# A transformer block in fp32 on one core: the first 352 columns of the input projection taken token tile by token tile

## The chip, the core and the metric

One NeuronCore of a Trainium2 chip runs the kernel. The metric is device time in microseconds (us), the median of the runs shown. Engines: TensorE (PE; its weight loads are PEld), VectorE (DVE), ScalarE (ACT), GpSimd (POOL) and SyncE (SP), each with a queue of its own; DMAs are issued from the queues of SP and ACT.

## What is computed

One hybrid encoder block on x of 1024 tokens by 1024 features, all in fp32. The part that matters here is its beginning:

```python
h = rms_norm(x, norm_mix_pre[l])          # per token: x * rsqrt(mean(x^2) + eps) * gain
z = h @ w_in[l]                           # 1024 x 1024 by 1024 x 2816
# columns of z: attention q (512), k (128), v (128); retention q, k, v, gate (512 each)
a = window_attention(rope(aq), rope(ak), av, attn_sink[l])
r = retention(rq, rk, rv, rg, ...)
x = x + rms_norm(concatenate([a, r]) @ w_out[l], norm_mix_post[l])
```

Behind it come cross-attention into 256 memory tokens and a SwiGLU feed-forward layer, which the change leaves alone.

## The kernel before

Tokens lie in 8 tiles of 128 (`NT`), features in 8 tiles of 128 (`NK`). A product in fp32 accuracy is made of three matmuls in the reduced fp32r format (`three`, lines 495 to 497): both operands are split into a high part (rounded) and a low part (the rest), and hi by hi, hi by lo and lo by hi are added up in PSUM. PSUM has 8 banks of 128x512.

The normalized x must be transposed before it can be the stationary operand. For a token tile t: ScalarE sums the squares (line 833) and takes the root (835), VectorE inverts it (1145) and scales the tile (1165), TensorE transposes eight 128x128 blocks into two PSUM banks (`turn_rows`, 491), ScalarE copies them out as `t_hi` (`hi_parts`, 843), VectorE subtracts for `t_lo` (`lo_parts`, 1152). x lies in the first 1024 columns of `z`, which the projection later overwrites.

The projection's 2816 columns are done in 8 pieces (`ZP`) of 352 columns (`ZW`). Per piece the 8 weight tiles (128x352) pass through a ring of four slots (`RING`): SP loads `raw` (341), GpSimd makes `w_hi` (398) and `w_lo` (402), TensorE multiplies. `product` goes weight tile by weight tile (k outside) and within it over the 8 token tiles, each with a bank of its own; so a piece can start only when all 8 token tiles are transposed and split, and it holds all 8 banks. ScalarE evicts the banks at the piece's end (876). The order is hand-written: each engine runs its own list, and semaphores tie them (`w_loaded` per slot, `w_rounded`, `w_split`, `w_used`, `tile_done`, `turned`, `act_ev`, `dve_ev`, `scaled`).

SP's queue begins with x tile 0, four weight tiles, x tiles 1 to 7. ScalarE issues the nine loads of constants (862 to 872) behind the last high part of x.

## Time and profile before

| | us |
|---|---|
| median of 3 runs | 1686.9 |
| the runs | 1686.15, 1686.9, 1692.22 |
| span of the profiled execution | 1681.7 |

The profiled execution's span runs from its first to its last instruction; what lies around it is in the runs' times and not in the span. Its mean granted TensorE clock was 0.968 of full. The page gives the busy time of each engine over the span, and the same in 40 slices. The timeline gives instructions in order of time, with the idle time before one and what ended it in brackets. Matmul ends are modelled and overlap, so the spacing of the starts is what counts, not the durations. The windows view gives busy time and granted clock of a stretch. The chain view follows back what ended last.

### The profile page before, as it was taken

To read this page: it belongs to the slowest core of one execution; us is meant where nothing else is said; L and a number is where in the kernel's file an instruction comes from. 1 tells how busy PE (TensorE), PEld (TensorE's weight loads), DVE (VectorE), ACT (ScalarE), POOL (GpSimd) and SP (SyncE) were. 2 spreads that over 40 slices of the span, in tenths; PEclk is the share of its full clock that TensorE was granted. 3 is DMA by queue.
4 is the path that set the end of the run, shared out by engine and by line. 5 is a ranking of instruction groups with operands and counts; after the bars stand their busy time and mean duration, and the time that the engine had idled before them with its cause. 6 is when DMAs were issued, how large, how long until landed. Compare 5 with 4: busy or idle time off the path is not lost.

```text
span 1681.7 us, 20944 instructions
## 1 busy us (share of the span) xinstructions
PE 1597.8 (95%) x7656; PEld 1329.0 (79%) x7656; DVE 584.5 (35%) x1022; ACT 373.2 (22%) x814; POOL 690.4 (41%) x580
## 2 busy tenths in 40 slices
PE   5999999899979999998998999999999999999995
PEld 4999999678968777875686788888888888888884
DVE  5061075455850820024138103214124042141237
ACT  5001014445432651133045100101101001011013
POOL 2444452200646575420356444434343434343435
PEclk7999999699979999999998999999999999999998
DMA  5111111000041042100011111111111111111112
GB/s 195 50 45 50 47 44 39 1 1 1 13 174 65 26 150 101 44 32 1 29 48 38 44 44 50 45 50 44 50 44 50 44 50 44 50 44 47 46 31 100
DMA packets 57236, 86.96 MB, mean 52 GB/s; under 512 B 5600, under 2 KB 36576, under 8 KB 57184
## 3 DMA queue, kind: packets, MB, share of 16 engines
q1 hardware_dynamic: 53312, 75.52, 14.6%
q10 hardware_dynamic: 3872, 10.76, 1.8%
q8 instruction: 31, 0.51, 0.1%
q14 instruction: 21, 0.17, 0.0%
HBM read 82.06 MB, written 4.19 MB: 51 GB/s over the span
## 4 chain that ended last, share of the span: by engine, by line
PE 91%; DVE 3%; ACT 3%; issue 1%; POOL 1%; DMA 0%; POOLq 0%; DVEq 0%; ACTq 0%
PE ps L495 26%; PE ps L496 26%; PE ps L497 25%; PE ps L491 4%; PE ps L614 3%; PE ps L588 3%; PE ps L760 2%; PE ps L671 1%; PE ps L649 1%; ACT px L1078 1%; DVE t_lo L1152 1%; DVE px L1400 1%; DVE wmx L1390 0%; PE ps L738 0%; DVE z L1165 0%
## 5 line engine op out<-in xcount | busy, mean ns | idle before, releaser
L398 POOL TENSOR_TENSOR w_hi<-raw,zero 128x512 fp32r<-128x512 f32 (+1 forms) x244 | 242.0, 992 | 719.9 <-PE ps L497 713.3
L495 PE MATMUL ps<-t_hi,w_hi 128*128 128x512 f32 x832 | 330.1, 397 | 4.2 <-DVE t_lo L1152 1.6
L496 PE MATMUL ps<-t_lo,w_hi 128*128 128x512 f32 x832 | 329.8, 396 | 0.0
L497 PE MATMUL ps<-t_hi,w_lo 128*128 128x512 f32 x832 | 329.8, 396 | 0.0
L402 POOL TENSOR_TENSOR w_lo<-raw,w_hi 128x512 fp32r<-128x512 f32 (+1 forms) x244 | 304.5, 1248 | 19.1
L495 PE MATMUL ps<-w_hi,t_hi 128*128 128x352 f32 (+1 forms) x768 | 268.1, 349 | 4.6 <-DVE t_lo L1152 3.1
L496 PE MATMUL ps<-w_lo,t_hi 128*128 128x352 f32 (+1 forms) x768 | 268.2, 349 | 0.0
L497 PE MATMUL ps<-w_hi,t_lo 128*128 128x352 f32 (+1 forms) x768 | 267.6, 348 | 0.0
L495 PEld LDWEIGHTS ps<-t_hi,w_hi 128*128 128x128 f32 x832 | 156.7, 188 | 43.2 <-DVE t_lo L1152 1.8
L1437 DVE TENSOR_TENSOR gs<-gs,ps 128x512 f32<-128x512 f32 x44 | 30.3, 688 | 451.4 <-ACT gs L1116 407.6
L497 PEld LDWEIGHTS ps<-t_hi,w_lo 128*128 128x128 f32 x832 | 156.7, 188 | 38.2
L496 PEld LDWEIGHTS ps<-t_lo,w_hi 128*128 128x128 f32 x832 | 156.7, 188 | 38.0
L1116 ACT ACTIVATE gs<-ps 128x512 f32<-128x512 f32 x44 | 26.3, 599 | 645.0 <-PE ps L497 645.0
L495 PEld LDWEIGHTS ps<-w_hi,t_hi 128*128 128x128 f32 x768 | 145.7, 190 | 18.0 <-DVE t_lo L1422 2.2
L497 PEld LDWEIGHTS ps<-w_hi,t_lo 128*128 128x128 f32 x768 | 145.5, 189 | 11.5
L496 PEld LDWEIGHTS ps<-w_lo,t_hi 128*128 128x128 f32 x768 | 145.5, 189 | 11.5
L1464 DVE TENSOR_TENSOR y<-ps,y 128x512 f32<-128x512 f32 x160 | 109.7, 691 | 87.9 <-PE ps L497 86.8
L496 PE MATMUL ps<-w_lo,f_hi 128*128 128x512 f32 x352 | 139.9, 397 | 0.0
L495 PE MATMUL ps<-w_hi,f_hi 128*128 128x512 f32 x352 | 138.9, 395 | 0.5 <-POOL w_lo L402 0.5
L497 PE MATMUL ps<-w_hi,f_lo 128*128 128x512 f32 x352 | 138.5, 394 | 0.0
L450 POOL TENSOR_TENSOR x<-x,y 128x1024 f32<-128x1024 f32 x24 | 57.3, 2386 | 73.1 <-DVE y L1356 73.1
L495 PEld LDWEIGHTS ps<-w_hi,f_hi 128*128 128x128 f32 x352 | 66.1, 188 | 17.6 <-POOL w_lo L402 0.9
(154 smaller groups left out, 1743.7 us busy)
## 6 DMA issues: line engine op xcount, KB each, us to landing
raw<-in_ffn_w_gu_dram SPq DMA_DIRECT2D x88, 256.0 KB, 3.1
raw<-in_w_in_dram SPq DMA_DIRECT2D x64, 176.0 KB, 2.3
raw<-in_ffn_w_down_dram SPq DMA_DIRECT2D x44, 256.0 KB, 2.6
raw<-in_xa_wkv_dram SPq DMA_DIRECT2D x32, 256.0 KB, 3.2
z<-in_x_dram SPq DMA_DIRECT2D x8, 512.0 KB, 8.1
raw<-in_w_out_dram SPq DMA_DIRECT2D x16, 256.0 KB, 2.6
x<-in_x_dram ACTq DMA_DIRECT2D x8, 512.0 KB, 8.0
raw<-in_xa_wq_dram SPq DMA_DIRECT2D x16, 256.0 KB, 2.7
```

The lines of the kernel that those rows point to most:

```text
L398: nc.gpsimd.tensor_tensor(hi[:, s, 0:width], raw[:, s, 0:width], zero[:, 0:1].broadcast_to([P, width]), ALU.add).then_inc(w_rounded, 1)
L402: nc.gpsimd.tensor_tensor(lo[:, s, 0:width], raw[:, s, 0:width], hi[:, s, 0:width].bitcast(F32), ALU.subtract).then_inc(w_split, 1)
L450: nc.gpsimd.tensor_tensor(x1[:, t, :], x1[:, t, :], y[:, t, :], ALU.add).then_inc(added, 1)
L491: return nc.tensor.transpose(ps[:, b, col:col + P], src, ident[:, :])
L495: nc.tensor.matmul(out, a_hi, b_hi, start=start, stop=False)
L496: nc.tensor.matmul(out, a_hi, b_lo, start=False, stop=False)
L497: return nc.tensor.matmul(out, a_lo, b_hi, start=False, stop=stop)
L588: nc.tensor.matmul(ps[:, j, 0:(k1 - k0) * P], qT[g * AD:(g + 1) * AD, j, n * P:(n + 1) * P], kT[g * AD:(g + 1) * AD, k0 * P:k1 * P], start ...
L614: last = nc.tensor.matmul(ps[:, 7, h * AD:(h + 1) * AD], pTw[:, j, kb * P:(kb + 1) * P], z[:, k0 + kb, C_V + g * AD:C_V + (g + 1) * AD], s ...
L760: last = nc.tensor.matmul(ps[:, 6 + d % 2, :], vM[:, mm, d * P:(d + 1) * P], pTx[:, mm, d // 2, :], start=mm == 0, stop=mm == NM - 1)
L1437: nc.vector.tensor_tensor(gs[:, p, :], gs[:, p, :], bank(2 * p + 1), ALU.mult).then_inc(dve_ev, 1)
L1464: nc.vector.tensor_tensor(v, bank(t), v, ALU.add).then_inc(dve_ev, 1)
```

## The change

The first piece (columns 0 to 351) is taken out of the loop and goes token tile by token tile. It needs all 8 weight tiles on chip at once: weight tiles 0 to 3 are split into a second ring, `w_hi3`/`w_lo3`, laid over room that is free at that time, and tiles 4 to 7 into the usual ring. Their raw data: tiles 0 to 3 in `raw`, tiles 4 to 7 in unused columns of `z`. SP loads all 8 weight tiles ahead of x tiles 1 to 7. ScalarE rounds them (it was GpSimd), GpSimd only subtracts. x is transposed through banks 4 to 7, and the first piece's tiles take banks 0 to 3 in turn, evicted by ScalarE as they are done (`first_out`, counted by `z0_out`). ScalarE starts with a Sqrt of a constant. The second piece is written out ahead of the loop, which now runs from 2. VectorE subtracts tile 0's low parts at once and those of the others one tile late, as before. The loads of constants on ScalarE's queue stay behind its x work, which now holds the evictions of the first piece too.

```diff
@@ -62,7 +62,7 @@
 TURNED = dict(x=0, qk=16, c=42, mem=58, h2=62, k=78, h3=82)
-ACT_EV = dict(x=0, z=16, qk=80, c=93, o=109, mem=125, h2=129, kv=145, k=153, q=157, xo=173, h3=189, end=205)
+ACT_EV = dict(x=0, z=8, qk=72, c=85, o=101, mem=117, h2=121, kv=137, k=145, q=149, xo=165, h3=181, end=197)
 DVE_EV = dict(x=0, qk=16, c=29, mem=45, h2=49, h3=65, end=81)
 TILES = dict(z=0, o=56, kv=70, q=74, xo=88, f=102)
@@ -77,6 +77,8 @@
 def turn_bank(n):
+    if n < TURNED["qk"]:
+        return 4 + n % 4
     if n < TURNED["mem"]:
         return (n - (TURNED["c"] if n >= TURNED["c"] else 0)) % 8
     return 4 + (n - (TURNED["h3"] if n >= TURNED["h3"] else TURNED["h2"] if n >= TURNED["h2"] else TURNED["mem"])) % 4
@@ -199,6 +201,7 @@
         Z = overlay(
             [("z", [P, NT, IN_COLS], F32), ("ropet", [P, 2 * NT * (AD // 2 + RD // 2)], F32),
              ("rope_a", [P, D], F32), ("rope_b", [P, D], F32)],
+            [("z_3", [P, NT, IN_COLS], F32), ("w_hi3", [P, RING, 512], F32R), ("w_lo3", [P, RING, 512], F32R)],
             [("z_1", [P, NT, IN_COLS], F32), ("junk_c", [P, 1536], F32), ("qtab", [P, RH, 2, P], F32),
              ("pTw", [P, G, 3 * P], F32)],
             [("z_2", [P, NT, IN_COLS], F32), ("junk_d", [P, 1536], F32), ("qtab_1", [P, RH, 2, P], F32),
@@ -233,10 +237,12 @@
         w_loaded = [sem(f"w_loaded{i}") for i in range(RING)]
+        w_first = [sem(f"w_first{i}") for i in range(RING)]
         w_rounded = sem("w_rounded")
         mem_rounded = sem("mem_rounded")
         w_split = sem("w_split")
         w_used = sem("w_used")
+        z0_out = sem("z0_out")
         tile_done = sem("tile_done")
         turned = sem("turned")
         act_ev = sem("act_ev")
@@ -320,6 +326,15 @@
         def bank(b, n=512):
             return ps[:, b, 0:n]
+        def first_raw(k):
+
+            return raw[:, k, 0:ZW] if k < RING else z[:, k - RING, 2 * D:2 * D + ZW]
+
+        def first_split(k):
+
+            hi, lo = (w_hi3, w_lo3) if k < RING else (w_hi, w_lo)
+            return hi[:, k % RING, 0:ZW], lo[:, k % RING, 0:ZW]
+
         def qk_dst(i):
             g, c = i // 2, slice(i % 2 * 512, (i % 2 + 1) * 512)
@@ -335,20 +350,19 @@
         @block.sync
         def _(sp):
-            def load(u, k, dst, src, first=False):
-                if not first:
-                    sp.wait_ge(w_split, u + (k - RING + 1))
+            def load(u, k, dst, src):
+                sp.wait_ge(w_split, u + (k - RING + 1))
                 sp.dma_start(dst, src).then_inc(w_loaded[k % RING], 16)
-            def piece(u, view, cols, width, first=False):
+            def piece(u, view, cols, width):
                 for k in range(NK):
-                    load(u, k, raw[:, k % RING, 0:width], view[k, :, cols], first and k < RING)
-                    if first and k == RING - 1:
-                        for t in range(1, NT):
-                            sp.dma_start(z[:, t, 0:D], x_v[t]).then_inc(x_in[t], 16)
+                    load(u, k, raw[:, k % RING, 0:width], view[k, :, cols])
             sp.dma_start(z[:, 0, 0:D], x_v[0]).then_inc(x_in[0], 16)
-            piece(U_Z, win_v, slice(0, ZW), ZW, True)
+            for k in range(NK):
+                sp.dma_start(first_raw(k), win_v[k, :, 0:ZW]).then_inc((w_loaded if k < RING else w_first)[k % RING], 16)
+            for t in range(1, NT):
+                sp.dma_start(z[:, t, 0:D], x_v[t]).then_inc(x_in[t], 16)
             with sp.Fori(1, ZP) as c:
                 piece(c * NK + U_Z, win_v, bass.ds(c * ZW, ZW), ZW)
             with sp.Fori(0, 2) as c:
@@ -387,14 +401,13 @@
         @block.gpsimd
         def _(pool):
-            def split(u, u0, k, width, first=False, loads=None, hi=w_hi, lo=w_lo, used=None):
+            def split(u, u0, k, width, loads=None, hi=w_hi, lo=w_lo, used=None):
                 s = k % RING
                 w_used_up = u + (k - RING + 1) if used is None else used
-                n = 16 * ((u0 + k) // RING + 1)
+                n = 16 * ((u0 + k) // RING)
                 pool.wait_ge(w_loaded[s], n if loads is None else loads * 16 + n)
-                if not first:
-                    pool.wait_ge(w_used, w_used_up)
+                pool.wait_ge(w_used, w_used_up)
                 nc.gpsimd.tensor_tensor(hi[:, s, 0:width], raw[:, s, 0:width],
                                         zero[:, 0:1].broadcast_to([P, width]), ALU.add).then_inc(w_rounded, 1)
@@ -404,8 +417,12 @@
             pool.wait_ge(set_up, 1)
             for k in range(NK):
-                split(U_Z, U_Z, k, ZW, k < RING)
-            with pool.Fori(1, ZP) as c:
+                hi, lo = first_split(k)
+                pool.wait_ge(w_rounded, k + 1)
+                nc.gpsimd.tensor_tensor(lo, first_raw(k), hi.bitcast(F32), ALU.subtract).then_inc(w_split, 1)
+            for k in range(NK):
+                split(NK + U_Z, U_Z, k, ZW, loads=2, used=k + 1 if k < RING else None)
+            with pool.Fori(2, ZP) as c:
                 for k in range(NK):
                     split(c * NK + U_Z, U_Z, k, ZW, loads=c * 2)
@@ -544,12 +561,37 @@
             pe.wait_ge(ident_in, 16)
-            for t in range(NT):
-                turn_rows(t, lambda j: z[:, t, j * P:(j + 1) * P], 2 * (t % 4),
+            def turn_x(t):
+                turn_rows(t, lambda j: z[:, t, j * P:(j + 1) * P], 4 + 2 * (t % 2),
                           lambda: pe.wait_ge(scaled, t + 1),
-                          lambda half: pe.wait_ge(dve_ev, 2 * (t - 4) + half + 1) if t >= 4 else None)
-            pe.wait_ge(dve_ev, DVE_EV["qk"])
-            with pe.Fori(0, ZP) as c:
+                          lambda half: pe.wait_ge(dve_ev, 2 * (t - 2) + half + 1) if t >= 2 else None)
+
+            def first_piece(t):
+                pe.wait_ge(dve_ev, 2 * t + 2)
+                if t >= 4:
+                    pe.wait_ge(z0_out, t - 3)
+                order = range(NK) if t < NT - 1 else [*range(RING, NK), *range(RING)]
+                for n, k in enumerate(order):
+                    if t == 0:
+                        pe.wait_ge(w_split, k + 1)
+                    hi, lo = first_split(k)
+                    last = three(ps[:, t % 4, 0:ZW], t_hi[:, k, t * P:(t + 1) * P], t_lo[:, k, t * P:(t + 1) * P],
+                                 hi, lo, n == 0, n == NK - 1)
+                    if t == NT - 1:
+                        last.then_inc(w_used, 1)
+                    elif n == NK - 1:
+                        last.then_inc(tile_done, 1)
+
+            turn_x(0)
+            first_piece(0)
+            turn_x(1)
+            for t in range(1, NT):
+                if t + 1 < NT:
+                    turn_x(t + 1)
+                first_piece(t)
+            product(NK + U_Z, NT, ZW, lambda t: pe.wait_ge(z0_out, t + 5) if t < 4 else None,
+                    rows_by_weights(t_hi, t_lo, ZW))
+            with pe.Fori(2, ZP) as c:
                 product(c * NK + U_Z, NT, ZW,
                         lambda t: pe.wait_ge(act_ev, c * NT + (ACT_EV["z"] - NT + t + 1)),
                         rows_by_weights(t_hi, t_lo, ZW))
@@ -853,11 +895,35 @@
             act.dma_start(gain_a[:, :], rows(norm_mix_pre)).then_inc(ga_in, 16)
             act.dma_start(ident[:, :], identity).then_inc(ident_in, 16)
             act.wait_ge(set_up, 3)
-            for t in range(NT):
+            nc.scalar.activation(rms[:, 63:64], eps[:, 0:1], ACT.Sqrt)
+
+            def row_sums(t):
                 square_root(t, z[:, t, 0:D], z[:, t, D:2 * D], D, lambda: act.wait_ge(x_in[t], 16))
-                if t:
-                    hi_parts(TURNED["x"] + 2 * (t - 1), t_hi, (t - 1) * P)
+
+            def first_round(k):
+                act.wait_ge((w_loaded if k < RING else w_first)[k % RING], 16)
+                nc.scalar.activation(first_split(k)[0], first_raw(k), ACT.Copy).then_inc(w_rounded, 1)
+
+            def first_out(t):
+                tile_ready("z", 0, t, NT, U_Z)
+                nc.scalar.activation(z[:, t, 0:ZW], bank(t % 4, ZW), ACT.Copy).then_inc(z0_out, 1)
+
+            row_sums(0)
+            for k in range(RING):
+                first_round(k)
+            hi_parts(TURNED["x"], t_hi, 0)
+            for k in range(RING, NK):
+                first_round(k)
+            row_sums(1)
+            first_out(0)
+            for t in range(2, NT):
+                row_sums(t)
+                hi_parts(TURNED["x"] + 2 * (t - 1), t_hi, (t - 1) * P)
+                if t >= 3:
+                    first_out(t - 2)
             hi_parts(TURNED["x"] + 2 * (NT - 1), t_hi, (NT - 1) * P)
+            for t in range(NT - 2, NT):
+                first_out(t)
             act.dma_start(sink[:, :], rows(attn_sink)).then_inc(c_in, 16)
             act.dma_start(dec[:, 0:RH], rows(ret_decay_fwd)).then_inc(c_in, 16)
@@ -870,7 +936,7 @@
             act.wait_ge(scaled, NT)
             act.dma_start(gain_a[:, :], rows(norm_mix_post)).then_inc(ga_in, 16)
-            with act.Fori(0, ZP - 1) as c:
+            with act.Fori(1, ZP - 1) as c:
                 for t in range(NT):
                     tile_ready("z", c, t, NT, c * NK + U_Z)
                     nc.scalar.activation(z[:, t, bass.ds(c * ZW, ZW)], bank(t, ZW), ACT.Copy).then_inc(act_ev, 1)
@@ -999,7 +1065,7 @@
                 nonlocal rounds
                 for _ in range(min(n, 4 * NK - rounds)):
                     u, slot = U_KV + rounds, (U_KV + rounds) % RING
-                    act.wait_ge(w_loaded[slot], 16 * (u // RING + 1))
+                    act.wait_ge(w_loaded[slot], 16 * (u // RING))
                     act.wait_ge(w_used, u - RING + 1)
                     nc.scalar.activation(w_hi[:, slot, :], raw[:, slot, :], ACT.Copy).then_inc(mem_rounded, 1)
                     rounds += 1
@@ -1164,7 +1230,9 @@
                 invert(t)
                 nc.vector.scalar_tensor_tensor(out=z[:, t, 0:D], in0=z[:, t, 0:D], scalar=rstd[:, t:t + 1],
                                                in1=gain_a[:, :], op0=ALU.mult, op1=ALU.mult).then_inc(scaled, 1)
-                if t:
+                if t == 0:
+                    lo_parts(ACT_EV["x"], TURNED["x"], t_hi, t_lo, 0)
+                elif t >= 2:
                     lo_parts(ACT_EV["x"] + 2 * (t - 1), TURNED["x"] + 2 * (t - 1), t_hi, t_lo, (t - 1) * P)
             lo_parts(ACT_EV["x"] + 2 * (NT - 1), TURNED["x"] + 2 * (NT - 1), t_hi, t_lo, (NT - 1) * P)
```

## Rows read from the trace of the kernel before

**Rows 1.** Page, busy time of each engine: us, share of the span, instructions.

```profile
PE 1597.8 (95%) x7656; PEld 1329.0 (79%) x7656; DVE 584.5 (35%) x1022; ACT 373.2 (22%) x814; POOL 690.4 (41%) x580
```

**Rows 2.** Timeline, all engines, 6 to 15 us: start, duration, engine, line, instruction.

```profile
6.10 1.28 ACT L833 ACT_TABLE_LOAD   x1 [6.10 <-DMA z<-in_x_dram]
...
7.92 0.93 POOL L402 TENSOR_TENSOR w_lo<-raw,w_hi 128x352 fp32r<-128x352 f32 x1
...
8.56 1.28 ACT L835 ACT_TABLE_LOAD   x1
...
10.05 1.04 ACT L833 ACTIVATE z<-z 128x1024 f32<-128x1024 f32 x1
...
11.85 1.60 DVE L1165 SCALAR_TENSOR_TENSOR z<-z,rstd,gain_a 128x1024 f32<-128x1024 f32 x1
...
12.45 1.80 POOL L402 TENSOR_TENSOR w_lo<-raw,w_hi 128x352 fp32r<-128x352 f32 x1
13.01 0.60 ACT L843 ACTIVATE t_hi<-ps 128x512 fp32r<-128x512 f32 x1 [1.50 <-PE ps L491]
...
14.50 0.69 DVE L1152 TENSOR_TENSOR t_lo<-ps,t_hi 128x512 fp32r<-128x512 f32 x1 [0.16 <-ACT t_hi L843]
```

**Rows 3.** Timeline, TensorE alone, 10 to 34 us: transposes, merged while they follow on.

```profile
11.89 3.65 PE L491 MATMUL ps<-ident,z 128*128 128x128 f32 x16 [11.89 <-DVE z L1165]
17.40 1.09 PE L491 MATMUL ps<-ident,z 128*128 128x128 f32 x8 [1.86 <-DVE z L1165]
19.98 1.97 PE L491 MATMUL ps<-ident,z 128*128 128x128 f32 x8 [1.49 <-DVE z L1165]
```

**Rows 4.** Windows view: busy time and count per engine, granted clock, DMA share, GB/s.

```profile
20.00:34.00 14.00, 9.83 (x40) 7.83 (x40) 12.52 (x20) 10.24 (x22) 0.00 (x0) 0.50 0.00 0
473.00:474.00 1.00, 1.00 (x7) 0.83 (x5) 1.00 (x3) 0.50 (x2) 0.67 (x1) 0.72 0.00 0
600.00:640.00 40.00, 40.00 (x205) 33.30 (x204) 7.53 (x13) 23.49 (x43) 32.04 (x27) 1.00 0.47 161
```

**Rows 5.** Timeline, TensorE alone, from 34 us: first piece, start of the second.

```profile
34.77 0.66 PE L495 MATMUL ps<-w_hi,t_hi 128*128 128x352 f32 x1 [1.74 <-DVE t_lo L1152]
...
40.16 0.32 PE L495 MATMUL ps<-w_hi,t_hi 128*128 128x352 f32 x1
...
68.00 0.32 PE L495 MATMUL ps<-w_hi,t_hi 128*128 128x352 f32 x1
```

**Rows 6.** Page, DMA issues: line, engine, count, KB each, us from issue to landing.

```profile
ropet<-const_rope_tables_dram ACTq DMA_DIRECT2D x1, 768.0 KB, 4.9
gain_a<-in_norm_mix_pre_dram ACTq DMA_DIRECT2D x1, 512.0 KB, 5.5
```

**Rows 7.** Timeline, 40 to 80 us, ScalarE's eviction and GpSimd's next split.

```profile
64.94 3.81 ACT L876 ACTIVATE z<-ps 128x352 f32 x8 [31.27 <-PE ps L497]
...
68.31 0.77 POOL L398 TENSOR_TENSOR w_hi<-raw,zero 128x352 fp32r<-128x352 f32 x1 [2.11 <-PE ps L497]
```

**Rows 8.** Timeline, TensorE alone, 625 to 628 us: transposes between two products.

```profile
625.66 1.91 PE L491 MATMUL ps<-ident,y 128*128 128x128 f32 x16
627.32 0.48 PE L495 MATMUL ps<-w_hi,m_hi 128*128 128x512 f32 x1
```

**Rows 9.** Timeline, VectorE alone, from 90 us: first use of the rotary tables.

```profile
96.21 1.38 DVE L1185 TENSOR_TENSOR rope_a<-z,ropet 128x640 f32<-128x640 f32 x1 [61.83 <-ACT z L876]
```

**Rows 10.** Chain of waits, attention stage, in order of time: start, us, what.

```profile
324.85 2.11 PE ps L491 x9
...
337.92 2.11 PE ps L491 x9
...
345.97 1.13 PE ps L491 x9
...
352.98 1.14 PE ps L491 x9
```

**Rows 11.** Timeline, TensorE alone, 466 to 474 us: transposes only.

```profile
468.55 5.52 PE L491 MATMUL ps<-ident,z 128*128 128x128 f32 x24 [5.45 <-POOL z L433]
```

More of the change, by code:

```diff
@@ L222, in build @@
         w_hi2, w_lo2 = Z["w_hi2"], Z["w_lo2"]
+        w_hi3, w_lo3 = Z["w_hi3"], Z["w_lo3"]
         kst = mem_t
```

## The prediction

> **What bounds the kernel now.** I began with the busy table of the page: TensorE is busy for 1597.8 us, 95% of the span of 1681.7 us [rows 1]. So a gain must come from TensorE's idle or slow stretches, and the change touches one of them, the first 68 us. The timeline of that stretch is the second view. x tile 0 is on chip at 6.1 us, but a table load stands there until 7.39 and a second one at 8.56 [rows 2]. TensorE then only transposes, eight transposes (8 of 128x128) at a time with waits between [rows 3], and works 9.83 of the 14 us from 20 to 34, at a granted clock of 0.50 [rows 4], which is the 1.2 GHz level of the two (1.2 and 2.4). The first product starts at 34.77 us. Its first 18 matmuls take until 40.16, 0.30 us each; the other 174 take until 68.00, 0.160 us each [rows 5]. At 68.00 the second piece starts, and from there TensorE runs without a gap. So the mark by which this change is to be judged is the start of the second piece: 68.0 us now.
>
> **The change part by part.** The order is now one chain between engines, so I follow it by durations of the rows.
>
> Tile 0, start. The dummy Sqrt loads its table set before x arrives. In the trace of before no load follows that of L835 in this stretch, although Square, Copy and Sqrt go on [rows 2]; so the set holds all three, and both loads leave the path. The sum of squares starts at 6.1. For tile 1 the scaling begins 11.85 - 10.05 = 1.80 us after the sum of squares [rows 2]; so here it begins at 7.9 and ends, at 1.28 us, at 9.2. The gain that it reads lands 5.5 us after its issue at 0.75, at 6.3 [rows 6]: not late. Transposes start at 9.3, ScalarE takes the first half 13.01 - 11.89 = 1.12 us later, and the second low part ends at 14.50 + 0.69 = 15.19, which is 3.3 us after the transposes began [rows 2, 3]. So tile 0 is ready at 12.6.
>
> The eight weight tiles. ScalarE now rounds them: four before tile 0's high parts (7.6 to 9.5) and four behind them (11.9 to 13.8). No row shows that copy from SBUF; the nearest is the 352 column copy out of PSUM, 3.81 us for 8, 0.48 each [rows 7]. Between 0 and double that price the later steps move little, since GpSimd is the slower one: its subtraction takes 0.93 us, but 1.80 where VectorE scales a tile at the same time [rows 2]. From 8.1: eight by 0.94 is 7.5, and two overlaps (the scaling of tile 0 at 7.9, of tile 1 at 15.6) by 0.95 each give 17.6 us. The bounds are 15.7 (no overlap) and 18.5 (three). In sentences of its own: the Trainium skill (SBUF — State Buffer, section "SBUF: two separate sides") says that of a GpSimd operation and a VectorE operation with two SBUF inputs the later one is blocked until the first ends. By that rule the two overlaps would cost up to 1.28 each and not 0.95, the end would be 0.7 us later, and the sum below 0.7 us larger. The row shows a GpSimd operation lengthened by 0.87.
>
> Tile 0's 24 matmuls are thus paced by the weights; the last three (0.30 each) end at 18.5.
>
> The link to tile 1. ScalarE has summed tile 1's squares at 15.2, then waits for tile 0's product to evict it. Behind that wait stands the sum of squares of tile 2; behind that the transposes of tile 2, which TensorE must do before tile 1's product. Eviction starts 0.31 us after a product's end (GpSimd's release at 68.31 against 68.00) and takes 0.48 [rows 5, 7]: 19.3. Scaling begins 1.80 later and takes 1.28: 22.4. The transposes of tile 2 start at 22.5. They take 1.97 us at the low clock, 1.09 at the high one [rows 3]; the low parts of tile 1 end beside them (22.4 + 1.28 = 23.7). I take the low clock, because TensorE stands idle for about 2 us just here, and in the trace of before the clock fell between 17.40 and 19.98 amid such transposes. So tile 1's product starts at 24.5. Bounds: 21.4 (weights at 15.7, high clock) and 27 (three overlaps, one more wait of 1.5).
>
> From there TensorE has 7 tiles of 24 matmuls: 168 by 0.160 is 26.9 us. Between them stand five more groups of eight transposes. In a stage where transposes stand between products, 16 of them start at 625.66 and the next product at 627.32, 0.83 us for eight [rows 8]; I take 0.92 with the longer first matmul behind them, 4.6 us in all.
>
> Clock. Products began at 34.77 and the clock rose at about 40.1, 5.3 us later [rows 5]. Counted from 22.5 it rises at 27.8. Then 3.3 us of product run at 0.30 instead of 0.16 us each and cost 1.5 us; bounds 0 (never fell) and 3.
>
> Does something starve TensorE in this stretch? After a product's end ScalarE evicts (0.31 + 0.48), sums squares, and the scaling ends at +3.9 us, the low parts behind it at +5.2. TensorE needs the first at 0.92 + 3.84 = +4.8 and the second at +5.7. So 0.5 us of slack is left per tile. I take 0; 0.5 us per tile late would be 3 us.
>
> The sum: 24.5 + 26.9 + 4.6 + 1.5 = 57.5 us against 68.0, a gain of 10.5 us.
>
> At the seam nothing is late. GpSimd splits the second piece's first tile within the last token tile: released 0.48 + 0.31 after its start, ready at about +2.6, needed at +3.84. Bank 3 is evicted 0.8 us after the end and needed 1.44 us after it. On SyncE's queue four more weight tiles (0.7 MB) now stand ahead of x tile 1. It was on chip by 10.05 [rows 2], when x tiles 0 and 1, the gain and four weight tiles had come, 2.2 MB; a third more is at most 3.2 us, and it is now asked for at 13.8, just not late. Weight tiles 4 to 7 land before it, and ScalarE comes to them at 11.9. The nine constant loads on ScalarE's queue move from 33 to about 58 us, behind the last eviction; the rotary tables take 4.9 us to land [rows 6] and are wanted at 96.2 now [rows 9], about 86 then. Without that cover of 20 us they would cost their own landing. The unrolled second piece issues the same instructions.
>
> Time: the median of 1686.9 lies 5.2 us above the profiled span; span and median should fall alike, the span to about 1671.2 and the time to 1676.4 us.
>
> **The rivals.**
>
> A, the attention stage moves its clock. From about 303 to 340 us the attention steps run at the low clock though TensorE is never idle. There a step takes 337.92 - 324.85 = 13.07 us; at the high clock 352.98 - 345.97 = 7.01 [rows 10]. One cold step more or fewer is 6.06 us. The three runs shown differ by just that: 1692.22 - 1686.15 = 6.07. So which step warms is a matter of alignment, and a shift of 10 us may change it. One step fewer gives 1670.3 us, one more 1682.5. For it speaks that spread; against a systematic change, that two runs and the profile agree.
>
> B, ScalarE's chain binds. If the slack of 0.5 us is used up, by GpSimd's or a semaphore's delays, and each of six tiles loses 0.8 us, 4.8 us go and the time is 1681.2.
>
> C, on the other side: the clock stays low through the whole tile-by-tile piece, since it is cut by transposes and waits. Then 168 matmuls cost 0.135 us more each (22.7 us), five groups of transposes 1.97 instead of 0.92 (5.3), less the 1.5 counted: 26.5 us. The second piece would start at 84, and the time is 1702.9. The gain of 10.5 is used up once 78 matmuls beyond the 11 counted run cold, somewhat over three token tiles. For it: the clock 0.50 from 20 to 34 in transposes with gaps [rows 4], and 37 us of busy attention at 0.50. Against it: from 600 to 640 us, with transposes between products, the clock was 1.00 [rows 4]. In sentences of their own: the Trainium skill (TensorE: Matmul & The Clock Gate, Part 4, PE-mode transpose) says that full clock "doesn't engage" in transpose mode, which isn't counted as busy in the same way. By that rule this rival has its mechanism. The trace bears it out only in part: 24 transposes in a row from 468.55 [rows 11] ended with the clock risen within 473 to 474 (mean 0.72 [rows 4]).
>
> D, the fall never happens, or GpSimd isn't hindered: tile 1's product starts near 21.4, with no cold stretch, 21.4 + 31.5 = 52.9, a gain of 15 us: 1671.8.
>
> E, nothing is gained because tile 0 is held up: TensorE reaches tile 1's product only at 35. That needs x or weights 10 us later than the rows have them; 1686.9.
>
> **How the numbers follow.** Forecast 1676.4 us with 0.50 (its own range, by the bounds on tile 1's start, the clock and the slack, 1672 to 1681), A fewer 0.11, A more 0.14, B 0.10, C 0.06, D 0.07, E 0.02. Range 1668 to 1685 us: it holds all but C, E and the edges. This kernel's measurement can tell about 0.5%, 8.4 us, from no change, so faster means under 1678.5. Of the forecast three quarters lie below that (0.38), with A fewer and D, and a little of the others: 0.58. Slower over 0.5% is C and a double A: 0.07. Within is the rest, 0.35.
>
> **What the profile after would show.** Start of ScalarE's first sum of squares at 6.1 with no table load before it; tile 0's products from 12.6 to 18.5, paced by GpSimd's subtractions; tile 1's product from 24.5; the clock back at about 28; products in runs of 3.84 us with 0.9 us of transposes between; the start of the second piece at 57.5; from there every stage 10.5 us earlier, and attention cold for four steps as before. The forecast is wrong if the clock reads 0.50 beyond 30 us, if TensorE waits on VectorE's low parts between tiles, or if the later stages don't keep the lead.

## The result and the profile after

| | before, us | changed, us |
|---|---|---|
| median of 4 runs each | 1686.53 | 1663.66 |
| the runs | 1679.02 to 1692.22 | 1661.31 to 1665.89 |
| span of the profiled execution | 1681.7 | 1660.8 |
| its own time | not recorded | 1662.83 |

The changed kernel is faster: ratio 0.9891, 95% interval 0.9864 to 0.9917, which is 14 to 23 us; 0.9891 is 18.4 us, and the two medians are 22.9 apart. The forecast was 1676.4 us, a gain of 10.5, in a range from 1668. The sign was right; the gain was 1.8 times the forecast by the ratio and 2.2 times by the medians, and the median lies 4 us under the range. In the recorded executions the time is 1.8 to 2.0 us above the span, so the profiled execution of before took about 1683.5 us (an estimate from its span). Two of the ten runs of b_shift10 below took 2019.73 and 2023.54 us at a mean granted clock of 0.74 and are left out of its median.

The page of the changed kernel: its span, TensorE's busy time, and the granted clock in 40 slices.

```profile
span 1660.8 us, 20839 instructions
...
PE 1583.9 (95%) x7656; PEld 1318.8 (79%) x7656; DVE 585.2 (35%) x1022; ACT 374.3 (23%) x822; POOL 684.6 (41%) x572
...
PEclk9999999699999999999998999999999999999998
```

Before, the row of the clock had a 7 in the first slice (0 to 42 us) and one in the twelfth (462 to 504 us, transposes ahead of the output projection); both are gone. The 6 of the attention stage in the eighth is still there. The timeline of TensorE at the start (start, duration, line, instruction, count, idle before), which answers to [rows 3, 5]:

```profile
9.22 1.94 PE L508 MATMUL ps<-ident,z 128*128 128x128 f32 x8 [9.22 <-DVE z L1231]
12.57 0.66 PE L512 MATMUL ps<-w_hi,t_hi 128*128 128x352 f32 x1 [1.41 <-DVE t_lo L1218]
...
16.17 0.32 PE L512 MATMUL ps<-w_hi,t_hi 128*128 128x352 f32 x1
...
17.63 0.32 PE L512 MATMUL ps<-w_hi,t_hi 128*128 128x352 f32 x1
...
18.12 1.03 PE L508 MATMUL ps<-ident,z 128*128 128x128 f32 x8
21.72 1.09 PE L508 MATMUL ps<-ident,z 128*128 128x128 f32 x8 [2.56 <-DVE z L1231]
22.91 0.66 PE L512 MATMUL ps<-w_hi,t_hi 128*128 128x352 f32 x1
...
26.30 0.33 PE L514 MATMUL ps<-w_hi,t_lo 128*128 128x352 f32 x1
...
28.38 1.04 PE L508 MATMUL ps<-ident,z 128*128 128x128 f32 x8
29.18 0.41 PE L512 MATMUL ps<-w_hi,t_hi 128*128 128x352 f32 x1
```

and the start of the second piece, which answers to the last of [rows 5]:

```profile
55.90 0.32 PE L512 MATMUL ps<-w_hi,t_hi 128*128 128x352 f32 x1
```

ScalarE over the same stretch, against [rows 2, 7], and GpSimd's eight subtractions:

```profile
6.01 1.06 ACT L875 ACTIVATE z<-z 128x1024 f32<-128x1024 f32 x1 [2.83 <-DMA z<-in_x_dram]
...
7.39 1.71 ACT L905 ACTIVATE w_hi<-raw 128x352 fp32r<-128x352 f32 x4
...
11.69 1.64 ACT L905 ACTIVATE w_hi<-z 128x352 fp32r<-128x352 f32 x4
...
18.32 0.46 ACT L909 ACTIVATE z<-ps 128x352 f32<-128x352 f32 x1 [3.62 <-PE ps L514]
...
56.10 0.47 ACT L909 ACTIVATE z<-ps 128x352 f32<-128x352 f32 x1 [3.39 <-PE ps L514]
```

```profile
8.02 4.51 POOL L422 TENSOR_TENSOR w_lo<-raw,w_hi 128x352 fp32r<-128x352 f32 x4 [7.56 <-ACT w_hi L905]
12.49 4.61 POOL L422 TENSOR_TENSOR w_lo<-z,w_hi 128x352 fp32r<-128x352 f32 x4
```

The sum of squares starts at 6.01 us with no load before it. Tile 0's product starts at 12.57. Its first 12 matmuls come 0.29 us apart and those from 16.17 on 0.16 us, so the clock rose in it; it ends at 18.1, and tile 0 is evicted at 18.32. TensorE waited for no weight tile in it: the last subtraction ends at 17.10, and the matmuls that need it start at 17.63. Tile 1's product starts at 22.91, at first at the low clock (0.29 to 0.30 us a matmul) and from 26.30 at the high one. From there it is product and transposes without idle time, as the windows view has it (TensorE busy for 29.70 of 29.70 us, granted clock 1.00):

```profile
26.30:56.00 29.70, 29.70 (x199) 29.59 (x199) 11.88 (x18) 13.06 (x28) 3.01 (x4) 1.00 0.01 2
```

The second piece starts at 55.90 us, where it was 68.00. That is 12.1 us.

The span fell by 20.9. The rest is in later stages, which no line of the change touches. I put the two traces beside each other by the starts of their stages. The largest difference is in the attention stage. The chain of waits there (start, us, what), against [rows 10]:

```profile
302.22 1.47 PE ps L508 x6
...
312.74 2.11 PE ps L508 x9
...
321.33 1.13 PE ps L508 x9
...
328.33 1.14 PE ps L508 x9
```

and the windows view of the changed kernel around it (columns as in [rows 4]):

```profile
289.00:316.00 27.00, 24.86 (x80) 17.97 (x81) 11.05 (x34) 11.59 (x40) 6.37 (x6) 0.50 0.00 1
316.00:400.00 84.00, 83.96 (x541) 66.40 (x540) 48.40 (x163) 40.07 (x137) 0.00 (x0) 1.00 0.00 1
```

The step that begins at 312.74 is the first with nine transposes, and the clock rises within it: the next comes 8.6 us later, the one behind it 7.0. In the trace of before the step at 324.85, at the same place of the program, ran wholly at the low clock and took 13.07 [rows 10]. From the first probabilities to the first retention product it is 111.65 us against 117.2, so 5.5 of the 20.9 us are here. Another 3.8 come from the stages from the retention's end to the cross-attention's scores, in which the clock fell and rose at other moments, and 0.6 are lost behind them: 12.1 + 5.5 + 3.8 - 0.6 is 20.8, the rest is rounding.

### The profile page after: what moved, and what is told of

Its sections match the earlier page's. It is cut to its first block, busy times and chain, and to the rows that moved or that the text cites. A ratio compares the mean times of both kernels' runs of the same rounds, so it can differ in the third digit from the quotient of the medians.

```text
span 1660.8 us, 20839 instructions
## 1 busy us (share of the span) xinstructions
PE 1583.9 (95%) x7656; PEld 1318.8 (79%) x7656; DVE 585.2 (35%) x1022; ACT 374.3 (23%) x822; POOL 684.6 (41%) x572
## 4 chain that ended last, share of the span: by engine, by line
PE 91%; DVE 3%; ACT 3%; issue 1%; POOL 1%; DMA 0%; POOLq 0%; DVEq 0%; ACTq 0%
PE ps L512 26%; PE ps L513 26%; PE ps L514 26%; PE ps L508 4%; PE ps L656 3%; PE ps L630 3%; PE ps L802 2%; PE ps L713 1%; PE ps L691 1%; ACT px L1144 1%; DVE t_lo L1218 1%; DVE px L1468 1%; DVE wmx L1458 0%; PE ps L780 0%; DVE y L1424 0%
## 5 line engine op out<-in xcount | busy, mean ns | idle before, releaser
L411 POOL TENSOR_TENSOR w_hi<-raw,zero 128x512 fp32r<-128x512 f32 (+1 forms) x236 | 234.8, 995 | 704.8 <-PE ps L514 704.8
L415 POOL TENSOR_TENSOR w_lo<-raw,w_hi 128x512 fp32r<-128x512 f32 (+1 forms) x236 | 297.0, 1259 | 18.5
L1182 ACT ACTIVATE gs<-ps 128x512 f32<-128x512 f32 x44 | 26.3, 599 | 645.0 <-PE ps L514 645.0
L512 PEld LDWEIGHTS ps<-w_hi,f_hi 128*128 128x128 f32 x352 | 66.1, 188 | 17.6 <-POOL w_lo L415 0.9
```

Source lines behind the costliest of these rows:

```text
L411: nc.gpsimd.tensor_tensor(hi[:, s, 0:width], raw[:, s, 0:width], zero[:, 0:1].broadcast_to([P, width]), ALU.add).then_inc(w_rounded, 1)
L415: nc.gpsimd.tensor_tensor(lo[:, s, 0:width], raw[:, s, 0:width], hi[:, s, 0:width].bitcast(F32), ALU.subtract).then_inc(w_split, 1)
L512: nc.tensor.matmul(out, a_hi, b_hi, start=start, stop=False)
```

## The experiments

The first question was the 12.1 us: what they are made of. The second was the other 9: does the change bring them, or did the two executions compared happen to differ? The columns on stages are read from each kernel's one profiled execution. A time is the median of four to eight runs made beside the kernel before on the same chip, or one run where the table says so.

Names with a_ are the changed kernel with an edit, those with b_ the kernel before with one; _again is another execution.

| kernel | second piece starts | one piece | first probabilities to retention | span | time |
|---|---|---|---|---|---|
| before | 68.0 | 30.72 | 117.2 | 1681.7 | |
| before_again | 68.2 | 31.15 | 112.0 | 1677.0 | 1678.8, one run |
| b_shift10 | 69.0 | 30.72 | 111.5 | 1673.8 | 1679.95 |
| b_preload | 65.9 | 30.72 | 123.2 | 1685.1 | 1686.9, one run |
| b_fill | 67.7 | 31.36 | 100.7 | 1668.7 | 1670.99 |
| b_fill_again | 68.2 | 31.15 | 100.7 | 1667.4 | 1669.18 |
| after | 55.9 | 30.72 | 111.65 | 1660.8 | 1663.66 |
| after_again | 55.5 | 30.72 | 111.55 | 1660.3 | 1665.18 |
| a_shift12 | 57.3 | 30.72 | 117.0 | 1670.8 | 1670.24 |
| a_poolround | 60.4 | 31.15 | 106.6 | 1664.8 | 1666.6, one run |
| a_sums2 | 53.0 | 31.15 | 117.1 | 1669.5 | 1666.94 |
| a_fill | 55.1 | 30.72 | 100.7 | 1652.9 | 1655.70 |
| a_fill_again | 56.2 | 30.72 | 100.7 | 1655.0 | 1657.0, one run |
| a_fill_sums2 | 52.9 | 31.15 | 100.7 | 1654.4 | 1656.14 |

The stage from the first down projection of the feed-forward part to the end is 670.5 to 670.6 us in all of them. The kernel before beside them had medians of 1686.53, 1681.06, 1681.14 and 1681.18 us (4, 18, 11 and 10 runs).

### Twelve more matmuls, and ten: does a shift alone change the attention stage?

```diff
+            pe.wait_ge(w_split, NK + U_Z + 1)
+            for _ in range(12):
+                nc.tensor.matmul(ps[:, 4, 0:ZW], t_hi[:, 0, 0:P], w_hi[:, 0, 0:ZW], start=True, stop=True)
             product(NK + U_Z, NT, ZW, ...
```

The changed kernel, with the second piece pushed back (a_shift12):

> The changed kernel with twelve extra 128x352 matmuls put in front of the second piece, results overwritten; nothing else is changed: 1.9 us at the high clock, so the second piece starts at 57.8 instead of 55.9 us. Theory L (alignment repeats from run to run): attention lies to the clock's changes as in before, one more cold step: 1663.7 + 1.9 + 5.5 = 1671.1 us, and up to 1674.4 with the 3.3 us of the transposes ahead of the output projection. Rival R (chance, or a property of the change): 1665.6 us.

Measured: 1670.24 us, ratio to before 0.9929 (0.9902 to 0.9956), against 0.9891 of the changed kernel. TensorE's timeline shows the twelve matmuls and then the second piece:

```profile
55.40 2.08 PE L594 MATMUL ps<-w_hi,t_hi 128*128 128x352 f32 x12
57.31 0.32 PE L512 MATMUL ps<-w_hi,t_hi 128*128 128x352 f32 x1
```

and the groups of transposes of the attention steps:

```profile
314.08 2.18 PE L508 MATMUL ps<-ident,sm 128*128 128x128 f32 x9
...
327.15 2.18 PE L508 MATMUL ps<-ident,sm 128*128 128x128 f32 x9
...
335.02 1.20 PE L508 MATMUL ps<-ident,sm 128*128 128x128 f32 x9
```

The step from 314.08 now takes 13.07 us at the low clock, and only the next one is shortened. So 1.9 us of added work came with 5.3 us more in the attention stage. That spoke for theory L. The counterpart, the kernel before with ten such matmuls in front of its first piece (b_shift10; the same three lines, with `range(10)` and a wait for the first weight tile):

> The kernel before with ten extra 128x352 matmuls of the first piece's shape put in front of the first piece, results overwritten; nothing else is changed. They cost ten places of 0.160 us, 1.6 us, at the start of the second piece (68.0 to 69.6). The before trace has the attention stage at the low clock from 303 to 340 us, the after trace from 291 to 316 us. Theory L (the clock's changes keep their times from the kernel's start from run to run, and what decides is how the attention steps lie to them): 1.6 us later is an alignment near the one of after, so attention rises one step earlier and the time falls in spite of the added work: 1686.5 + 1.6 - 5.5 = 1682.6 us, and 1679.3 if the transposes ahead of the output projection (460 to 490 us) also fall as in after. Rival R (which step warms is chance in every execution, or belongs to the change itself): 1688.1 us, in the spread of before.

Measured: 1679.95 us, ratio 0.9995 (0.9968 to 1.0023). Its profiled execution, the fastest of the eight, has the fast attention stage:

```profile
325.78 2.18 PE L491 MATMUL ps<-ident,sm 128*128 128x128 f32 x9
...
334.26 1.20 PE L491 MATMUL ps<-ident,sm 128*128 128x128 f32 x9
```

But its times lie in the same groups as those of before. The kernel before itself, in 18 runs beside it, had eight between 1680.3 and 1681.3, five from 1686.4 to 1689.0, and single ones at 1675.2, 1678.2, 1679.3, 1683.5 and 1692.5; the kernel with ten more matmuls had seven from 1675.6 to 1682.4 and one at 1692.5. So theory L fails in its strict form: the same program draws a different alignment in different executions. What remains of it is that a step at the low clock more or less is worth 5 to 6 us (the attention stage took 106.6, 111.6, 117.1 or 123.2 us in the table), near the distance of those groups. The clock's changes themselves differ within one program: the first rise came at 40.16 us in the first execution of before and at 39.00 in the second.

### The changed kernel again

> The changed kernel unaltered, in five rounds beside the kernel before. The profiles of the first comparison split the gain into 12.1 us by which the second piece starts earlier (68.0 to 55.9) and 8.8 us of less time at the low clock in the attention stage and in the transposes ahead of the output projection; the kernel before has since run at 1675 to 1692 us, in groups about 6 us apart, with a median of 1681. Theory J (the second part is chance of that comparison, each execution drawing its own alignment): the ratio moves towards 12.1 us alone, 0.993, with the changed kernel's runs spread over groups like those of before (1663, 1669, 1675). Rival S (the shift gives the later stages a better alignment for good): the ratio stays at 0.989 and the changed kernel stays near 1663.

Measured: 1665.18 us (1662.3 to 1669.5), before 1681.14 (1678.2 to 1689.6), ratio 0.9908 (0.9887 to 0.9930), a gain of 15.5 us. This lies between the two theories. The first comparison had met the kernel before in its upper groups (three of four runs at 1686 or more); over all later runs its median is 1681. The changed kernel keeps to 1661 to 1669.5 in all ten runs, and both profiles have 111.6 us of attention. The start gives 12.4 of them (68.1 in the mean of before and before_again, 55.7 in that of after and after_again). Some 3 us are then left. The profiles of before_again and after_again, 16.7 us apart in their spans, show where they lay in those two executions: 12.7 us at the start, 3.0 in seven pieces of 31.15 instead of 30.72 us, 0.4 in the attention stage and 0.6 behind it. More on the pieces follows.

### The attention stage at the high clock

Nine matmuls whose results are overwritten go into the wait ahead of the first attention probabilities, in the changed kernel (a_fill) and in the kernel before (b_fill). The wait in the changed kernel is the 3.54 us of this line:

```profile
290.97 1.68 PE L508 MATMUL ps<-ident,sm 128*128 128x128 f32 x6 [3.54 <-ACT sm L984]
```

```diff
                 if s + 1 < steps:
                     scores(s + 1)
+                if s == 0:
+                    for _ in range(9):
+                        nc.tensor.matmul(ps[:, 7, 0:3 * P], qT[0:AD, 0, 0:P], kT[0:AD, 0:3 * P], start=True, stop=True)
                 for j in range(3):
                     turn_probs(s, j)
```

> The changed kernel with nine 64x384 matmuls (0.355 us each at the high clock, 3.2 us) put into TensorE's wait of 3.54 us ahead of the first attention probabilities; their results go to a free bank and are overwritten. Theory: the low clock of the attention stage (291 to 316 us in the trace of after) comes from that wait and stays by the low density of the steps; with the wait filled the clock stays at 1.00 and 25.4 us of steps take half, a gain of up to 12.7 us: 1651 us. Rival: the steps at the high clock are bound by ScalarE and VectorE at first, or the clock falls all the same: 1663.7 us or more.

> The kernel before with the same nine matmuls in the same wait. Theory: 37.2 us of attention at the low clock (303.07 to 340.3) take half, a gain of 18.6 us: 1668 us; then the difference to the changed kernel with the same fill is the shift of the second piece alone, 12.1 us, plus up to 3.3 us from the transposes ahead of the output projection. Rival (the change gives more than its 12.1 us by something in the attention stage itself): the difference stays at about 20 us.

Measured: 1655.70 us (ratio 0.9845, 0.9814 to 0.9877) with the change, 1670.99 (0.9932, 0.9908 to 0.9955) without; the expectations were 1651 and 1668. The windows view of a second execution of the filled changed kernel:

```profile
284.00:300.00 16.00, 15.52 (x74) 10.69 (x74) 10.39 (x34) 12.07 (x32) 9.89 (x8) 1.00 0.00 0
300.00:395.00 95.00, 94.58 (x615) 75.06 (x615) 55.12 (x185) 48.09 (x157) 0.00 (x0) 1.00 0.00 1
```

and the chain of the first one:

```profile
286.46 5.45 PE ps L668 x17
291.91 0.81 PE ps L508 x6
...
297.91 0.56 DVE sm L1307
...
304.22 1.13 PE ps L508 x9
```

The clock no longer falls, and the groups of transposes take 1.13 us instead of 2.11. From the first probabilities to the retention it is 100.7 us in every execution, whatever the alignment. The rival was right in part: between 297.91 and 300.34 the chain leaves TensorE for VectorE and ScalarE, so not all of the 12.7 us comes, and the fill lengthens the stretch ahead of the first probabilities by 1.6 us (8.50 against 6.86). The expectation had the price of the fill wrong: each of the nine matmuls stands as two records in the trace, 17 of the 18 records take 5.45 us in the chain, and 3.2 was expected for all; that is more than the wait of 3.54. Fewer of them were not tried. The stage lost 11.0 us (111.65 to 100.7) and 1.6 came back; the changed kernel's time fell by 8.0 us against its first median and by 9.5 against its second. With the attention stage out of the comparison the change still gave 15.3 us, not 20 and not 12.1.

> The kernel before with the nine filling matmuls, once more. Its first profile took 31.36 us a piece in the projection's loop where before and after took 30.72 (matmuls of 352 columns 163.3 ns apart instead of 160.0), 4.4 us over seven pieces, which muddies the comparison of the two filled kernels (1671.0 against 1655.7 us, 15.3 apart). Theory P (the wider spacing belongs to the program): 31.36 us a piece again and about 1671 us. Rival E (it belongs to the execution): pieces of 30.72 us, and about 1666.5 us, where the difference to the filled changed kernel would be 11 to 12 us.

> The changed kernel with the nine filling matmuls, once more, for a second profile: its pieces took 30.72 us. Theory P: 30.72 again, 1655 to 1658 us. Rival E: may be 31.1 to 31.4 us a piece, with 3 to 4 us more in all.

> The kernel before unaltered, for one more profile, to see what stage the groups of its times (1675, 1680.5, 1687, 1692.5 us) come from. Expected: the first piece starts at 34.8 us again and the stages without attention keep their lengths; the stretch from the first attention probabilities to the retention products is 111.6, 117.2 or 123.2 us long, in steps of about 6, and the time goes with it. Rival: the pieces of the projection differ in length between executions (30.72 or 31.1 to 31.4 us) and carry the groups.

Measured: 1669.18 (five runs, ratio 0.9917, 0.9888 to 0.9947), 1657.01 and 1678.76 us (one run each). The evictions at the ends of the pieces tell the piece's length. Before, a second execution:

```profile
65.09 3.86 ACT L876 ACTIVATE z<-ps 128x352 f32 x8 [30.74 <-PE ps L497]
96.23 3.87 ACT L876 ACTIVATE z<-ps 128x352 f32 x8 [27.27 <-PE ps L497]
```

The changed kernel:

```profile
83.56 3.82 ACT L942 ACTIVATE z<-ps 128x352 f32 x8 [27.00 <-PE ps L514]
114.27 3.83 ACT L942 ACTIVATE z<-ps 128x352 f32 x8 [26.89 <-PE ps L514]
```

31.14 us a piece against 30.71. The kernel before took 30.72 in its first profile (95.65 - 64.94 there), so the same program has both; the filled one has 31.36 and 31.15. Theory P falls, since the length changed from one execution to the next; rival E's 30.72 us did not come either. In before_again the attention stage was 112.0 us as expected, but the first product started at 35.42 and not at 34.8, and the pieces had the length that its rival named. The wider spacing (162.2 or 163.3 ns instead of 160.0 between matmuls of 352 columns) holds for a whole execution, and it is in no stage with 512 columns. Over seven pieces it is 3.0 or 4.5 us. It does not settle the filled pair's 15.3 us to the last part. The spans of the first profiles are 15.8 apart: 12.5 at the start and 4.5 in the pieces, less 1.2 behind the attention stage. Those of the second are 12.4 apart: 12.0 and 3.0, less 2.6. What lies behind the attention stage has no lasting sign in the traces (3.2 us for the change in the first comparison, 0.6 in the second, 1.2 and 2.6 against it here), and the two filled kernels' second times are 12.2 us apart, one of them a single run. The five executions with the changed start unaltered (after, after_again, a_shift12, a_fill, a_fill_again) had the narrow spacing; three of the six with the old start, and all three with an edited changed start (a_poolround, a_sums2, a_fill_sums2), had the wide one. Whether the program has a part in which one it draws, these runs don't settle, so these 3 us are not credited to the change.

### The start, part by part

Only the Sqrt of a constant, put first on ScalarE in the kernel before:

```diff
             act.wait_ge(set_up, 3)
+            nc.scalar.activation(rms[:, 63:64], eps[:, 0:1], ACT.Sqrt)
             for t in range(NT):
```

> The kernel before with only the Sqrt of a constant put first on ScalarE, no reordering. Both table loads (1.28 us each) leave the way of x tile 0. Theory: that part alone brings the first piece forward by 0.8 to 2.5 us (34.77 to about 32.3 if every x tile is on chip in time, 34 if x tile 1 is not), since ScalarE and the transposes are then bound by their own chain; the second piece starts at 65.5 to 67.2 instead of 68.0. Rival: nothing moves, because the later x tiles set the time; 68.0.

ScalarE's timeline and TensorE's first product:

```profile
6.18 1.06 ACT L833 ACTIVATE z<-z 128x1024 f32<-128x1024 f32 x1 [3.00 <-DMA z<-in_x_dram]
...
9.83 1.06 ACT L833 ACTIVATE z<-z 128x1024 f32<-128x1024 f32 x1 [2.18 <-DMA z<-in_x_dram]
```

```profile
33.19 0.66 PE L495 MATMUL ps<-w_hi,t_hi 128*128 128x352 f32 x1 [1.70 <-DVE t_lo L1153]
```

Tile 0 starts 1.2 us earlier and needs no second load, but ScalarE then waits 2.18 us for x tile 1, which lands at 9.8. The first product moves from 34.77 to 33.19, the second piece from 68.0 to 65.9. So 2.1 of the 12 us can be had without the new order; its one time (1686.9) shows nothing of them, because its attention stage took 123.2 us in that execution. The expectation was right; x tile 1 did hold it back, though by less than it allowed for.

GpSimd rounding the weights, as it did:

```diff
-                pool.wait_ge(w_rounded, k + 1)
+                pool.wait_ge((w_loaded if k < RING else w_first)[k % RING], 16)
+                nc.gpsimd.tensor_tensor(hi, first_raw(k), zero[:, 0:1].broadcast_to([P, ZW]), ALU.add).then_inc(w_rounded, 1)
+                pool.wait_ge(w_rounded, k + 1)
...
-            for k in range(RING):
-                first_round(k)
             hi_parts(TURNED["x"], t_hi, 0)
-            for k in range(RING, NK):
-                first_round(k)
```

> The changed kernel with the rounding of the first piece's eight weight tiles given back to GpSimd (0.77 + 0.94 us a tile instead of 0.94 on GpSimd beside 0.43 on ScalarE). Theory: tile 0's product is paced by GpSimd, so 8 by 1.71 from 7.0 plus two overlaps with VectorE of about 0.95 end at 22.6, tile 0's product at 23.1 instead of 18.1, and the second piece starts at 60.9 us instead of 55.9. Rival: the weights are not what holds tile 0 and the start moves by under 1 us.

```profile
19.51 0.66 PE L514 MATMUL ps<-w_hi,t_hi 128*128 128x352 f32 x1 [0.99 <-POOL w_lo L424]
...
22.99 0.66 PE L514 MATMUL ps<-w_hi,t_hi 128*128 128x352 f32 x1 [0.49 <-POOL w_lo L424]
...
24.04 1.91 PE L510 MATMUL ps<-ident,z 128*128 128x128 f32 x8
...
28.87 0.43 PE L514 MATMUL ps<-w_hi,t_hi 128*128 128x352 f32 x1
```

Tile 0's product waits for GpSimd at the last five weight tiles and ends at 24.0 (23.1 expected), tile 1's starts at 28.87, 6.0 us later than before the edit. None of tile 1's matmuls is at the low clock here, where the changed kernel had 11, which gives 1.5 back. The second piece starts at 60.4, 4.5 us later than 55.9. The division of the rounding is worth about a third of the gain at the start.

The sum of squares of tile 2 ahead of tile 0's eviction:

```diff
             row_sums(1)
+            row_sums(2)
             first_out(0)
             for t in range(2, NT):
-                row_sums(t)
+                if t > 2:
+                    row_sums(t)
```

> The changed kernel with one line of ScalarE's list moved: the sum of squares of token tile 2 ahead of the eviction of tile 0, so that it no longer stands behind the wait for tile 0's product. In the trace of after TensorE idles 2.56 us there and tile 1's product starts at 22.9. Expected: scaling of tile 2 is done before tile 0's product ends at 18.1, both groups of transposes follow at once (0.9 us each), tile 1's low parts end near 20.6, its product starts at 20.7, and the second piece at 53.7 us instead of 55.9 (half a us either way by when the clock rises). Total time 2.2 us less. Rival: something else (low parts, the clock) binds tile 1's product and the start of the second piece stays at 55.9.

Measured: tile 1's product starts at 21.43 us (20.7 expected, 22.91 without the edit) and the second piece at 53.0. Only half of the 2.9 us is the shorter link; the other half is that the clock did not fall, so that no matmul of tile 1 is at the low clock, where the changed kernel had 11 in the trace compared. But the time is 1666.94 (0.9911, 0.9886 to 0.9935), no better than 1665.18 of the changed kernel beside it. Its profiled execution, with 1671.52 us one of the two longest of its six, had the long pieces (3.0 us) and 117.1 us of attention (5.5). So the 2.5 to 2.9 us gained at the start can't be told in the whole.

Both edits together:

> The changed kernel with both edits: nine filling matmuls ahead of the first attention probabilities, and the sum of squares of token tile 2 ahead of the eviction of tile 0. The fill took 8 to 9 us off the changed kernel and kept TensorE's matmuls there fast; the moved sum brought the second piece from 55.8 to 52.9 us, but that program took 31.14 us a piece, which gave 3 us back. Expected if the two add up: 1655.7 - 2.9 = 1652.8 us; with the wider spacing of the pieces as in the kernel with the moved sum alone, 1655.9 us. Either way faster than both kernels.

```profile
18.46 1.91 PE L508 MATMUL ps<-ident,z 128*128 128x128 f32 x16
21.07 0.43 PE L512 MATMUL ps<-w_hi,t_hi 128*128 128x352 f32 x1 [0.70 <-DVE t_lo L1223]
```

16 transposes in a row, 0.70 us of idle time instead of 2.56, and tile 1's product at 21.07. Measured 1656.14 us, ratio 0.9831 (0.9803 to 0.9858). It beats both kernels clearly, by 25 and by some 9 us, and the filled kernel without it (0.9845) not measurably; its profile again has 31.15 us a piece, for which 1655.9 us was expected. Of these two edits only the fill shows in the time.

## Why the prediction was right, and where it fell short

- **The mark** was well chosen. No stage after it gained except through the clock or the spacing of the matmuls.
- **Tile 0's chain.** Sum of squares 6.1 forecast, 6.01 measured; ready at 12.6, product at 12.57; weights done 17.6, measured 17.1. The copy that no row showed took 0.41 to 0.43 us (1.71 for four), near the 0.48 taken. The 1.28 us of a scaling stood in no row shown; the trace of before has it in seven of the eight:

```profile
10.45 1.28 DVE L1165 SCALAR_TENSOR_TENSOR z<-z,rstd,gain_a 128x1024 f32<-128x1024 f32 x1
```

- **The end of tile 0's product** was hit by luck: 18.5 forecast, 18.1 measured. The forecast had it paced by the weights. But its own price of 0.30 us a matmul puts 24 of them from 12.6 to 19.8, behind the weights, and TensorE waited for no weight tile. It was paced by its own clock, which rose at 16.17, halfway; in a_fill it rose at 17.88 and the product ended at 18.86. The weights do pace it once GpSimd rounds them (a_poolround).
- **The link to tile 1.** Forecast: scaling of tile 2 ends at 22.4, transposes at the low clock, product at 24.5. Measured: 21.7, 1.09 us at the high clock, 22.91. This step was mis-sized by 1.6 us, half of it by the transposes: the forecast took the low clock for them because TensorE stands idle for about 2 us ahead. It did (2.56 us), but the clock fell only behind the transposes, at 22.9. The fast bound of 21.4 for this step is 21.7 by the forecast's own durations.
- **Clock.** 11 matmuls at the low clock forecast, 11 seen (22.91 to 26.30), 1.5 us. That they agree is luck too. The forecast counted 5.3 us from the start of TensorE's work to the rise, read from one execution. Counted from the first product it was 5.4 us in before, 3.6 in before_again and 3.4 in b_fill; and tile 1 had 9 such matmuls in after_again and none in a_fill.
- **Transposes and slack.** 0.80 us for eight and 0.1 behind them, 0.92 forecast. TensorE waited for nothing between tiles. The low parts end at 33.12 and are needed at 33.91, a slack of 0.8 us where 0.5 was forecast, and rival B is refuted.
- **The sum.** 57.5 forecast; 55.9, 55.5, 55.1 and 56.2 in four executions with this start. The direct gain is 12.1 to 12.4 us, not 10.5. Apart from what paces tile 0's product, the mechanism of the forecast is what the traces show; the way to tile 1's product came out 1.6 us too long.
- **From span to time.** The forecast took the 5.2 us between the median and the profiled span as fixed. In the recorded executions it is 1.8 to 2.0; the other 3.4 were the difference between the profiled execution and the median run.
- **Rival C** (the clock stays low) is refuted: from 26.3 on the matmuls are 0.160 us apart and the granted clock reads 1.00, with transposes in every gap. In a sentence of its own: by the rule of the Trainium skill (TensorE: Matmul & The Clock Gate, Part 4: PE-mode transpose) full clock doesn't engage in transpose mode; the trace disagrees for transposes between products, where eight took 0.80 us against 1.97 at the low clock.
- **Rival A** was the right mechanism with the wrong weight. I had it as a case beside the forecast, with the forecast's own gain at 10.5, and its fast side at 1670.3. In the first comparison it came true (5.5 us), together with a better start (1.6) and with alignments of smaller stages (3.8 less 0.6) that I had given no term. They lay on the same side, so the time fell under a range whose ends took them one at a time. None of the 8.7 us behind the start is shown to be the change's: the attention stage was 112.0 us in before_again and 117.0 in a_shift12. That before's median of three runs stood in the upper half of its own distribution could not be seen from three runs; beside its later median of 1681 the gain is 15.5 us.
- **The wide spacing of the matmuls of 352 columns** stood in no row of before and in no case of mine.

## What to carry to other kernels

Find the first moment from which the bound engine never waits again, and judge an edit of the start by how far that moment moves; a chain of durations along the engines gave it here within 2.4 us, two of its parts by luck. Time differences of a few us behind it can come from where the clock rises and falls: compare the stages of several executions before a change is credited with them. And a short wait ahead of a thin stage can cost more than its length: 3.5 us of idle time was followed by 14 to 50 us of attention at half clock (a_poolround, b_preload), and nine useless matmuls in it were worth 8 to 12 us.

## What the runs showed of the hardware beyond expectation

One program has matmuls of 352 columns 160.0 ns apart in one execution and 162.2 in another (pieces of 30.72 and 31.15 us for the kernel before), constant within the execution, while the stage from the first down projection on, in 512 columns, keeps its length to 0.1 us.

The granted clock in a profile can miss changes. In the changed kernel it reads 1.00 for 12 to 16 us, where the matmuls are 0.29 us apart. In the second profile of before, TensorE's eight transposes take the 1.97 us of the low clock,

```profile
20.67 1.97 PE L491 MATMUL ps<-ident,z 128*128 128x128 f32 x8 [0.62 <-DVE z L1165]
```

and the windows view says 1.00 for the stretch:

```profile
20.00:34.00 14.00, 9.90 (x41) 7.85 (x40) 12.68 (x20) 11.31 (x23) 0.00 (x0) 1.00 0.00 0
```

Durations of a known instruction are the safer reading.

A stage can be at the low clock although TensorE's records leave next to no gap: in the attention steps the busy time was 36.76 of the 37 us from 303 to 340 in before, at 0.50. The clock rose in a different step in different executions (106.6, 111.6, 117.1 and 123.2 us of the stage), in a_poolround already in the second step, and once up it stayed.
